# Output weights and first attention outputs loaded during attention: a change to a hybrid encoder layer on one core

## The reference

```python
proj = h @ w_in
y_a = swa_sink_attention(qa, ka, va, sinks) @ w_o_a        # 512 -> 1024
y_b = dsa_mla_attention(qb, c_kv, qi, k_idx, w_idx, w_uk, w_uv, topk) @ w_o_b   # 512 -> 1024
g = jax.nn.sigmoid(gates + b_gate)
mix = (g_a * y_a + g_b * y_b) @ w_out
h = layer_norm(DEEPNORM_ALPHA * h + mix, ln1_g, ln1_b)
ff = (jax.nn.silu(h @ w_ff_gate) * (h @ w_ff_up)) @ w_ff_down
return layer_norm(DEEPNORM_ALPHA * h + ff, ln2_g, ln2_b)
```

## Time and profile before

| | |
|---|---|
| three timed runs | 3716.02, 3720.32, 3728.04 us (median 3720.32) |
| the profiled execution's own time | 3714.49 us |
| its span, first to last instruction | 3712.3 us |
| mean granted TensorE clock | 0.971 |
| TensorE busy | 3477.2 us (94%) |
| DVE, ACT, POOL busy | 2223.8 (60%), 1922.6 (52%), 1695.6 (46%) us |
| attention ends, third stage begins | 1989.8 us from the span's start |

### The profile page before, as it was taken

The page is one execution under the profiler, slowest core; times in us unless marked ns, Lnnn a source line. Parts: engine busy times, 40 slices in busy tenths (PEclk is TensorE's granted clock), DMA queues, the critical chain, the costliest instruction groups (busy, mean ns, idle before and its releaser), DMA issues. The chain is left out here.

```text
span 3712.3 us, 52455 instructions
## 1 busy us (share of the span) xinstructions
PE 3477.2 (94%) x17866; PEld 2904.7 (78%) x17866; DVE 2223.8 (60%) x3097; ACT 1922.6 (52%) x3592; POOL 1695.6 (46%) x1806
## 2 busy tenths in 40 slices
PE   6998999889989999999997998999999999999997
PEld 5776777677767888988996777778887888888786
DVE  5236888787623565666543665774547545555867
ACT  3223787788635798887553332343334333344443
POOL 5242344765311222222003665656665666554756
PEclk9999999999969999999998999999999999999998
DMA  7344324332221111100005455654446444365663
GB/s 272 130 131 111 99 83 127 122 92 78 77 74 47 40 43 35 35 16 20 23 11 181 152 172 184 235 197 144 173 142 207 146 140 148 140 236 191 235 226 132
DMA packets 338457, 468.42 MB, mean 126 GB/s; under 512 B 23184, under 2 KB 225120, under 8 KB 334992
## 3 DMA queue, kind: packets, MB, share of 16 engines
q1 hardware_dynamic: 310064, 387.47, 32.1%
q10 hardware_dynamic: 28128, 77.60, 5.7%
HBM read 311.21 MB, written 153.78 MB: 125 GB/s over the span
## 5 line engine op out<-in xcount | busy, mean ns | idle before, releaser
L2601 POOL TENSOR_TENSOR ff_rounded_ring<-ff_raw,ff_rounded_ring 128x512 fp32r<-128x512 f32 x264 | 382.5, 1460 | 288.3 <-ACT ff_rounded_ring L2748 285.7
L99 PE MATMUL ff_bank<-ff_rounded_pair,ff_rounded_ring 128*128 128x512 f32 x1232 | 482.9, 392 | 13.1 <-POOL ff_rounded_ring L2601 8.1
L100 PE MATMUL ff_bank<-ff_rounded_pair,ff_rounded_ring 128*128 128x512 f32 x1232 | 481.3, 391 | 0.0
L101 PE MATMUL ff_bank<-ff_rounded_pair,ff_rounded_ring 128*128 128x512 f32 x1232 | 481.2, 391 | 0.0
L1771 PE MATMUL at_ctx<-at_p_t,at_c_nat 128*128 128x128 f32 (+1 forms) x2432 | 351.2, 285 | 7.8 <-ACT at_ctx_t L1884 7.0
L1771 PEld LDWEIGHTS at_ctx<-at_p_t,at_c_nat 128*128 128x128 f32 (+1 forms) x2432 | 306.1, 194 | 37.5 <-ACT at_ctx_t L1884 13.0
L1878 ACT ACTIVATE at_p_t<-at_turn 128x512 f32<-128x512 f32 (+4 forms) x416 | 213.0, 544 | 206.4 <-PE at_turn L1748 172.7
L2606 POOL TENSOR_TENSOR ff_rounded_ring<-ff_raw,ff_rounded_ring 128x512 fp32r<-128x512 f32 x154 | 212.1, 1383 | 177.5 <-ACT ff_rounded_ring L2798 177.5
L3029 DVE TENSOR_TENSOR ff_rounded_a_ring<-ff_f_q,ff_rounded_a_ring 128x512 fp32r<-128x512 f32 x154 | 211.5, 1385 | 132.4 <-ACT ff_rounded_a_ring L2790 131.4
L99 PEld LDWEIGHTS ff_bank<-ff_rounded_pair,ff_rounded_ring 128*128 128x128 f32 x1232 | 232.4, 189 | 65.4 <-POOL ff_rounded_ring L2601 11.1
L101 PEld LDWEIGHTS ff_bank<-ff_rounded_pair,ff_rounded_ring 128*128 128x128 f32 x1232 | 232.4, 189 | 48.8
(11 more groups left out here) (399 smaller groups left out, 9058.7 us busy)
## 6 DMA issues: line engine op xcount, KB each, us to landing
f_kept<-ff_resid SPq DMA_DIRECT2D x154, 256.0 KB, 2.8
ff_f_q<-f_kept ACTq DMA_DIRECT2D x12, 2816.0 KB, 10.9
pj_raw<-in_w_in SPq DMA_DIRECT2D x58, 512.0 KB, 4.4
proj<-se_row SPq DMA_DIRECT2D x104, 256.0 KB, 2.4
ff_raw<-in_w_ff_gate SPq DMA_DIRECT2D x22, 1024.0 KB, 10.8
ff_raw<-in_w_ff_up SPq DMA_DIRECT2D x22, 1024.0 KB, 6.2
ff_raw<-down_comb SPq DMA_DIRECT2D x88, 256.0 KB, 2.7
ff_raw<-in_w_ff_down SPq DMA_DIRECT2D x66, 256.0 KB, 3.3
```

The costliest lines, as they stand in the source:

```text
L99: pe.matmul(out, lhs_lo, rhs_hi, start=start, stop=False, skip_group_check=goes_on)
L100: pe.matmul(out, lhs_hi, rhs_hi, start=False, stop=False, skip_group_check=goes_on)
L101: return pe.matmul(out, lhs_hi, rhs_lo, start=False, stop=stop, skip_group_check=goes_on)
L2601: pool.tensor_tensor(ring[:, step % RING, 1, :].rearrange("p (k c) -> p k c", c=P), f_operand(it, q, m), f32(ring[:, step % RING, 0, :]).r ...
```

## The change

- Two tiles of 128 x 8 x 512 (16 KB a partition), `early[0]` and `early[1]`, are allocated at the far end of SBUF before attention (`far`).
- During attention SP loads columns 0 to 511 of `w_o_a` and `w_o_b` into `early[0]` (behind the value loads issued in iteration t = 5), and in iteration 6, behind a wait for the stores of four tiles, rows 0 to 511 of the first group's attention outputs into half of `early[1]`. The other half of `early[1]` holds attention's four `p_t` tiles.
- In the third stage `early[0]` is the first half of W_o (blocks 0 to 3), a new tile `w_o_second` the other (blocks 4 to 7, loaded at the stage's start); all eight contraction steps of a block now lie in one tile. `early[1]` is `att`. ACT loads only its second half for group 0.
- Splitting a block of W_o is one instruction of 1024 columns on ACT and one on POOL, in every group.
- The rings of the feed-forward part take the place of the two far tiles (`first.close()` frees them), and two of the three raw weight buffers lie in `att`; their first loads wait for DVE's `att_lo_ready` in place of POOL's `lo_ready`.

```diff
-        p_t = [s.sb(f"p_t{u}", [P, 4, P]) for u in range(PT)]
+        p_t = [early[1][:, KT // 2 + u, :].rearrange("p (m c) -> p m c", m=4) for u in range(PT)]
...
                     load_values(t + 1)
+                    if t == 5:
+                        for e, src in enumerate((w_o_a, w_o_b)):
+                            sp.dma_start(early[0][:, 4 * e:4 * e + 4, :], src.rearrange("(k p) c -> p k c", p=P)[:, :, 0:GROUP]).then_inc(early_loaded[0], 16)
+                    if t == 6:
+                        sp.wait_ge(attn_stored, 32 * TPG)
+                        sp.dma_start(early[1][:, 0:4, :], attn[0:512, 0:GROUP].rearrange("(k p) c -> p k c", p=P)).then_inc(early_loaded[1], 16)
...
+        first.close()
+        ring, a_ring = [s.far(name, [P, RING, 2, GROUP], F32R) for name in ("ring", "a_ring")]
...
-        w_o_half = [w_o_first[:, :, :], raw_all[:, 0:4 * D].rearrange("p (k c) -> p k c", c=D)]
+        w_o_part, att = [early[0][:, :, :], w_o_second[:, :, :]], early[1]
...
-        def block_parts(b):
...
-            dst = slice(0, KT // 2), slice(KT // 2, KT)
-            return [(d, h[:, :, b * P:b * P + P]) for d, h in zip(dst, w_o_half)]
+        def block_part(b):
...
+            return w_o_part[b // 4][:, :, b % 4 * P:b % 4 * P + P]
...
                     elif j < 2:
-                        for u in range(2):
-                            sp.wait_ge(lo_ready[u], use1(NG - 1, KT - 2 + u) + 1)
+                        sp.wait_ge(att_lo_ready, KT * NG)
...
-                load_w_o(0)
                 load_gates(0, 0)
                 load_gates(0, 1)
+                load_w_o(0)
                 load_w_o(1)
                 for n, v in enumerate((ln1_g, ln1_b)):
                     sp.dma_start(ln[n][:, :], v.to_broadcast([P, D])).then_inc(ln_loaded, 16)
-                load_w_o(2)
-                load_w_o(3)
...
-                        for d, src in block_parts(b):
-                            last = pool.tensor_tensor(as_k(w_lo[u])[:, d, :], src, as_k(f32(w_hi[u]))[:, d, :], ALU.subtract)
-                        last.then_inc(lo_ready[u], 1)
+                        pool.tensor_tensor(as_k(w_lo[u]), block_part(b), as_k(f32(w_hi[u])), ALU.subtract).then_inc(lo_ready[u], 1)
...
-                        for d, src in block_parts(b):
-                            last = act.activation(as_k(w_hi[u])[:, d, :], src, ACT.Copy)
-                        last.then_inc(hi_ready[u], 1)
+                        act.activation(as_k(w_hi[u]), block_part(b), ACT.Copy).then_inc(hi_ready[u], 1)
...
-                    for e in range(2):
+                    for e in range(0 if g else 1, 2):
                         act.dma_start(att[:, 4 * e:4 * e + 4, :], attn[e * 512:e * 512 + 512, g * GROUP:(g + 1) * GROUP].rearrange("(k p) c -> p k c", p=P)).then_inc(att_loaded[e], 16)
```

More of the change, by code:

```diff
@@ L84, in sb, with far @@
         return self.enter_context(self.nc.sbuf_tensor(f"{self.tag}_{name}", shape, dt))
+    def far(self, name, shape, dt=F32):
+        return self.enter_context(self.nc.sbuf_tensor(f"{self.tag}_{name}", shape, dt, side="right"))
     def ps(self, name, shape):
@@ L1330, in project_and_select, with attention @@
     return s.all_sems
-def attention(nc, proj, v_nat, wuk_t, w_uv, sinks, attn, c_kept, dist_kept, score, done_with):
+def attention(nc, proj, v_nat, wuk_t, w_uv, sinks, attn, c_kept, dist_kept, score, done_with, early, early_loaded, w_o_a, w_o_b):
     c_nat_kept, c_hi_kept, c_lo_kept = c_kept
@@ L2171, in mix_and_ffn @@
 def mix_and_ffn(nc, proj, attn, h0, h1_turned_d, h1_nat, comb, f_kept, down_comb, w_o_a, w_o_b, w_out, ln1_g, ln1_b, w_gate, w_up, w_down,
-                ln2_g, ln2_b, out, outer):
+                ln2_g, ln2_b, out, outer, first, early, early_loaded):
     with Scope(nc, "ff") as s:
@@ L2679, in high_att @@
                 def high_att(g, k):
-                    act.wait_ge(att_loaded[k // 4], 16 * (g + 1))
+                    if k < 4 and g == 0:
+                        act.wait_ge(early_loaded[1], 16)
+                    else:
+                        act.wait_ge(att_loaded[k // 4], 16 * (g + k // 4))
                     if g:
@@ L3307, in build @@
     dist_kept = nc.dram_tensor("dist_kept", (TILES, P, L), F32, kind="Internal").ap()
-    with Scope(nc, "out") as outer:
+    with Scope(nc, "out") as outer, Scope(nc, "early") as kept, Scope(nc, "early") as first:
         outer.sems("stored", TPG + 1)
+        early_loaded = kept.sems("loaded")
         with Scope(nc, "late") as s:
@@ L3314, in build @@
                                           late_score, w_uk, wuk_t)
+            early = [first.far(f"half{u}", [P, KT, GROUP]) for u in range(2)]
             if phases > 2:
-                attention(nc, proj, v_nat, wuk_t, w_uv, sinks, attn, c_kept, dist_kept, late_score, done_with)
+                attention(nc, proj, v_nat, wuk_t, w_uv, sinks, attn, c_kept, dist_kept, late_score, done_with, early, early_loaded, w_o_a[0], w_o_b[0])
         if phases > 3:
@@ L3323, in build @@
             mix_and_ffn(nc, proj, attn, h0, h1_turned, h1_nat, comb, f_kept, down_comb, w_o_a[0], w_o_b[0], w_out[0], ln1_g, ln1_b,
-                        w_ff_gate[0], w_ff_up[0], w_ff_down[0], ln2_g, ln2_b, out, outer)
+                        w_ff_gate[0], w_ff_up[0], w_ff_down[0], ln2_g, ln2_b, out, outer, first, early, early_loaded)
 _INS = ["x", "meta_tokens", "ln0_g", "ln0_b", "w_in", "b_gate", "kv_norm_g", "w_uk", "w_uv", "k_idx_g", "k_idx_b", "sinks",
```

30 lines of the change are left out of this document (15 added, 15 removed).

## The result

The changed kernel takes **3756.54 us** (median of five runs, 3752.37 to 3758.23). Five runs of the kernel before beside it have their median at 3718.82 (3716.02 to 3728.04). The medians are 37.7 us apart; the ratio is 1.0094, with a 95% interval of 1.0084 to 1.0105. The prediction said 3729 with a range up to 3741: right in direction, 27.5 us short. The profiled execution took 3754.6 us.

What follows compares the result with a forecast made beforehand. TensorE, busy 3477 of 3712 us, was taken as the bound. From the profiled 3714.5, -9.2 (start) and +18.0 (POOL's fused subtraction) gave 3723.3, or 3729 on the timed runs' scale; range 3713 to 3741.

Steps and rivals of the forecast that it cites:

- The start: Start of the third stage: early loads let TensorE begin 9.4 us earlier and finish the first weight block 9.2 us earlier.
- my bounds of 6.3 and 10.6: First weight block's gain: 6.3 us if the clock rises only at the block's end, 10.6 if up at once.
- The transfers: Loads moved into attention: covered by 13 us for some 6 us of transfer, cost 0, otherwise a few us once.
- POOL's fused instruction: Mixing stage, groups 1 to 3: POOL's 1024-column subtraction makes DVE wait longer, 6.0 us a group, 18 us in all.
- my four steps: Group 1, from DVE's last subtraction before it through tile 3: successive DVE delays bring TensorE out of the loop 6.0 us late.
- steps 2 and 3: Group 1, tile 0: DVE's scaling ends 3.2 us later; then L2928 takes 0.7 instead of 1.29, leaving 2.7 later.
- step 4: Tiles 1, 2 and 3 of a group: each DVE scaling waits 1.1 us more, 3.3 a group.
- the first line of "The rest": Rings and transposed-probability tiles moved to the far end of memory: the new address costs matmuls 0.
- DVE does not wait longer: Mixing stage: DVE gets in during POOL's 1024-column instruction, or slack absorbs the delay; 3711 us, chance 0.15.
- half of the delay: Mixing stage: only the longer scaling waits at tiles 1 to 3 count, 10 us in all; 3721 us, chance 0.10.
- The early loads do little: Third stage's start: the half loaded behind the barrier lands late, gain 3 us in place of 9; 3735 us, chance 0.05.
- The clock falls in the longer waits: Mixing stage: TensorE's longer waits lower its clock, 3 us a group behind the third wait; 3738 us, chance 0.18.

## Why the prediction was wrong

**The start was right**, a little less so in the first block. I had the first matmul 9.4 us earlier; it came 9.6 us nearer to attention's end and at 1997.04, where 1994.6 was named on the scale of before and attention ended 2.6 later. The chain of steps held as well: POOL and DVE take turns, and TensorE does its second step 1.06 us late. The gain at the block's end was to be 9.2. The last of its 24 matmuls, before and after:

```profile
2012.03 0.39 PE L101 MATMUL ff_bank<-ff_rounded_pair 128*128 128x512 f32 x1
```

```profile
2004.58 0.56 PE L104 MATMUL ff_bank<-ff_rounded_pair 128*128 128x512 f32 x1
2004.98 0.39 PE L102 MATMUL ff_bank<-ff_rounded_pair 128*128 128x512 f32 x1
...
2006.83 0.39 PE L104 MATMUL ff_bank<-ff_rounded_pair 128*128 128x512 f32 x1
```

From attention's last transposition that is 27.53 and 19.70 us, a gain of 7.8. It lies inside my bounds of 6.3 and 10.6: matmuls ran at the lower clock until 7.9 us after the first one (the one at 2004.58 is the last that takes longer), where I had carried over 5.9.

**The transfers cost nothing that these traces resolve**: attention took 0.3 us longer with the 3 MB that it loads beside its work. Over the fourteen executions it took between 934.7 and 940.2 us by the same measure, and 935.4, 936.9 and 939.9 in the three that have no early loads.

**POOL's fused instruction was right** in mechanism, and about right in size. +18 was predicted, the stage gave +20.0 in the pair of traces and 18.8 in the means over the fourteen. In group 1 the transpositions are 8.89, 9.32 and 9.30 us apart, where it was 6.36, 7.19 and 8.22, in sum 5.7 later against the 6.0 of my four steps; groups 2 and 3 give 5.8 each. DVE's scaling of tile 0, which took 1.28, shows steps 2 and 3:

```profile
2096.39 3.42 DVE L2958 SCALAR_TENSOR_TENSOR ff_resid<-ff_resid,ff_rstd,ff_ln 128x1024 f32<-128x1024 f32 x1 [0.46 <-POOL ff_rstd L2584]
```

Before, TensorE transposed tile 0 3.55 us behind the scaling's end (2101.84 to 2105.39), now 0.48 (2099.81 to 2100.29): 3.1 us of slack are used up there, and DVE's own steps from tile 0 to tile 3 are 2.7 longer (step 4 said 3.3). The run with only POOL split removes all of it, the one with only ACT split none. The rest of the +20.0 is none of this. Between the groups 0.7 and 0.8 us were won back, which my "nothing behind it is idle enough" had excluded, so that the three groups make 15.9; 1.8 more are there before the first transposition, from the start block above, and 2.3 behind the last one. The Trainium skill ("SBUF — State Buffer", sections Who interferes with whom and Summary: rules for kernel authors) states it as the rows show it: a DVE instruction with two SBUF inputs and a GpSimd instruction that reads SBUF exclude each other, and the second one is blocked until the first has finished. The measured end, 1.08 us behind POOL's, agrees.

**The step that failed** is the first line of "The rest": "what tile they read shows no price, and I take 0 for the address". It was worth +27.6 us, or 3696 products at 0.0075. The two rows on which it rested could not show a price, since both stand for matmuls whose two operands begin at the same remainder modulo 256: `ring`, the pairs and `a_ring` were laid out from the near end one behind the other, 16384 bytes each. The far end from which the allocator gives out tiles lies at 229344, which is 224 modulo 256, so a tile allocated from there does not share the remainder of those from the near end (128). The bound that I set for an unknown cost, none at all, was taken from rows that varied something else (which tile) and not the thing that the change altered (where tiles lie against each other). With 27.6 more, the prediction would have been 3757.

**The rivals.** *DVE does not wait longer* is refuted by the scaling line at 3.39 us, *half of the delay* by 5.7 us in group 1 and 18.8 in the stage where it gave 3.3 and 10. *The early loads do little* is refuted by the first matmul. *The clock falls in the longer waits*: it does fall, to 0.84 and 0.73 in the windows above, and matmuls of 0.77 us follow, but DVE sets the pace in that loop and a slower matmul hides in it: the transpositions of group 1 are 9.32 us apart with that fall between them and 9.30 with none. The price was to come behind the third wait of a group, 3 us each. From the transposition of tile 3 to that of the next group's tile 0 it took 73.36 and 86.09 us where it was 74.04 and 86.90, so behind groups 1 and 2 there is no such price. Behind group 3 the clock did fall:

```profile
2344.00:2348.00 4.00, 3.94 (x13) 3.21 (x14) 2.90 (x4) 2.55 (x4) 2.57 (x2) 0.72 0.61 176
```

From there to the first product it took 65.8 us instead of 63.5. That is at most 2.3 us for the clock behind these waits and not 9, and a wait at 2375.01 that grew from 0.66 to 2.45 us is in it too; no run isolates the clock's price alone. The Trainium skill ("TensorE: Matmul & The Clock Gate", section HAM oscillation) says that waits between bursts of matmuls can send the clock back each time. Here it went back in some of them only: six of the nine waits for DVE's scaling are of 1.9 us or more, and the clock falls with or behind four.

The chance of 0.08 for faster and the range up to 3741 took only waits and the clock into account. I had named "if the ring matmuls changed their duration" as what would make the prediction wrong, and gave it no price.

## What to carry to other kernels

Two tiles that meet in long matmuls, here of 512 columns, should begin at the same remainder modulo 256 bytes, and a tile that is moved or allocated from the other end of the memory should be looked at for that; a pad of 96 bytes was worth 30 us here. Joining two instructions into one can be a loss where another engine gets in between them only at instruction borders (18.8 us here), even if the engine that issues them has less to do. And where a trace shows no price for something, ask whether it varied what the change varies.

## What was not expected of the hardware

- One 512-column matmul of these fp32r tiles follows another after 0.2267 us when the starts of its stationary and moving operand are equal modulo 256, and 0.2324 to 0.2343 when they differ by 32, 64, 96 or 128 (0.229 in one pass of one stage), at a granted clock of 1.00 in all stretches shown. The rule was seen at differences in steps of 32 only, since the allocator rounds to these. Why the hardware does so is open: no run tells whether it is the reading of weights or of columns that stops.
- The 128-column matmuls of attention show no such price: `at_ctx` stays at 285 ns, and at 0.112 us from start to start (the median in both traces), with its stationary operand (`at_c_nat`) at 128 and the moving one (the probabilities) at 224 modulo 256, where both were at 128 before.
- With the operands 64 apart, the down products ran the first pass of the stage at 0.229 and the second, with the same instructions and the same remainders, at 0.233. Why is open.
